# Hybrid attention step: the schedule of the cached samples changed from nine slots to ten, and the value products from two pages to four at a time

## What is computed

```python
k_full = cache_k[page_table[:, :own_page0]]
k_mean = jnp.mean(k_full.reshape(DB, n_full, MOBA_BLOCK, H, hd), axis=2)
gate = jnp.einsum('bqhd,bnhd->bhqn', qf, k_mean)
_, sel = lax.top_k(gate, top)                 # 3 of 4 blocks
# p: softmax over the selected pages and the new token
out = jnp.einsum('bhqk,bhqkd->bqhd', p, v_sel)
```

## Time and profile before

| | before |
|---|---|
| median of 3 runs | 469.26 us |
| span of the profiled execution, first to last instruction | 467.2 us |
| median less span (the profiled execution has no time of its own beside its span in the results; this stands for what lies around it) | 2.06 us |
| TensorE busy | 456.2 us (98%) |
| VectorE busy | 394.1 us (84%) |
| ScalarE busy | 294.4 us (63%) |
| GpSimd busy | 100.9 us (22%) |
| moved by DMA | 150.91 MB, mean 323 GB/s |

### The profile page before, as it was taken

How to read it: one execution, slowest core, us unless ns; L and a number is a source line. 1 busy time by engine, 2 the same in 40 slices (tenths; PEclk the granted TensorE clock), 3 DMA queues, 4 the chain that set the end, 5 groups by cost and what they waited for, 6 DMA issues and landing times.

```text
span 467.2 us, 11345 instructions
## 1 busy us (share of the span) xinstructions
PE 456.2 (98%) x3855; PEld 413.8 (89%) x3855; DVE 394.1 (84%) x1610; ACT 294.4 (63%) x490; POOL 100.9 (22%) x181
## 2 busy tenths in 40 slices
PE   6999999999999999999999999999999999999997
PEld 4899899897879888888899889899898898899997
DVE  3898899699999799999899999799999774668861
ACT  4966545686984496995486695666948357324430
POOL 2040421013323213423321332321223110000000
PEclk9999999999999999999999999999999999999999
DMA  8899699749999999999999999998999985457511
GB/s 304 322 353 407 183 322 371 240 158 340 317 416 408 404 368 354 412 410 408 408 380 315 409 412 409 411 372 303 382 415 409 410 334 188 149 180 261 182 48 48
DMA packets 44858, 150.91 MB, mean 323 GB/s; under 512 B 6192, under 2 KB 7796, under 8 KB 44672
## 3 DMA queue, kind: packets, MB, share of 16 engines
q1 hardware_dynamic: 20368, 70.77, 40.8%
q0 software_dynamic: 19008, 67.20, 37.3%
q10 hardware_dynamic: 5424, 12.21, 6.8%
HBM read 137.37 MB, written 12.76 MB: 321 GB/s over the span
## 4 chain that ended last, share of the span: by engine, by line
PE 70%; ACT 10%; DVE 10%; DMA 4%; issue 4%; ACTq 1%; POOLq 0%; SPq 0%; POOL 0%; DVEq 0%
PE pj L534 28%; PE pj L537 13%; PE wk L534 6%; PE pa L717 4%; PE wk L537 3%; DMA kpages<-in_cache_k 3%; DVE kpages L1170 3%; DVE wlo L1071 2%; ACT L838 2%; ACT whi L818 2%; PE wk L487 2%; DVE cslot L1252 2%; PE wk L639 2%; PE wk L673 1%; DMA cst<-in_consts 1%
## 5 line engine op out<-in xcount | busy, mean ns | idle before, releaser
L534 PE MATMUL pj<-xn,whi 128*128 128x264 f32 x1328 | 180.8, 288 | 1.6 <-ACT mqT L976 1.3
L534 PEld LDWEIGHTS pj<-xn,whi 128*128 128x128 f32 x1328 | 168.4, 189 | 10.2 <-issue 6.2
L1071 DVE TENSOR_TENSOR wlo<-wraw,whi 128x1024 fp32r<-128x1024 f32 x112 | 136.1, 1220 | 8.8 <-ACT whi L818 8.3
L818 ACT ACTIVATE whi<-wraw 128x1024 fp32r<-128x1024 f32 x112 | 117.9, 1053 | 23.1 <-PE wk L537 12.9
L1170 DVE CUSTOM_DVE_ANT_0 kpages<-kpages,qbc 128x128 f32<-128x128 f32 x512 | 115.5, 292 | 5.3 <-DMA kpages<-in_cache_k 5.1
L537 PE MATMUL pj<-xn,wlo 128*128 128x264 f32 x664 | 93.8, 284 | 0.4 <-DVE wlo L1071 0.4
L537 PEld LDWEIGHTS pj<-xn,wlo 128*128 128x128 f32 x664 | 85.5, 188 | 0.6 <-DVE wlo L1071 0.6
L404 POOL DMA_DIRECT2D kpages<-in_cache_k x64 | 34.3, 536 | 165.9 <-DVE sco L1170 141.9
L404 POOL DMA_DIRECT2D vpages<-in_cache_v x64 | 33.9, 530 | 57.9 <-issue 38.9
L1170 DVE DVE_READ_ACCUMULATOR2_ANT sco<- 128x1 f32 x512 | 42.8, 84 | 0.0
L717 PE MATMUL pa<-vpages,prob 128*32 128x256 f32 x512 | 34.2, 385 | 1.7 <-ACT prob L876 1.7
(11 more groups left out here) (271 smaller groups left out, 615.0 us busy)
## 6 DMA issues: line engine op xcount, KB each, us to landing
wraw<-in_weights SPq DMA_DIRECT2D x112, 512.0 KB, 6.8
kpages<-in_cache_k POOLq DMA_DIRECT2D x64, 512.0 KB, 8.1
vpages<-in_cache_v POOLq DMA_DIRECT2D x64, 512.0 KB, 10.8
cslot<-in_states SPq DMA_DIRECT2D x16, 512.0 KB, 9.4
out_C_s<-cslot ACTq DMA_DIRECT2D x16, 512.0 KB, 8.1
xres<-in_tokens SPq DMA_DIRECT2D x1, 1056.0 KB, 5.5
out_k_p<-kT ACTq DMA_DIRECT2D x4, 256.0 KB, 10.2
out_v_p<-v_nat ACTq DMA_DIRECT2D x4, 256.0 KB, 4.7
```

Of the source, the lines that this page charges most:

```text
L534: mm(bank[:, 0:T], whi[:, q, k, :], src[:, g, k, :], start=(k == 0 and g == 0), stop=False)
L818: A(whi[:, n % WSPLIT], wraw[:, n % WRAW], ACT.Copy).then_inc(whi_ready, 1)
L1071: V.tensor_tensor(wlo[:, n % WRAW], wraw[:, n % WRAW], whi[:, n % WSPLIT], ALU.subtract).then_inc(wlo_ready, 1)
```

## The change

The formula for the slots becomes tables. Samples start every 10 slots (2, 12, ... 72), so slots 8 and 9 of each sample have no key page. A visit has four pages, and there are two a sample: at 13 and 17 after the start; at 13 and 14 for the seventh sample (slots 75, 76), at 11 and 12 for the last one (slots 83, 84). The last sample has a shorter chain: SUMS at 8, SELECT 9, SHIFT and EXP 10, TOTAL 11, GATHER 13 (slot 85, as before). Value pages are loaded one a slot from slot 14 on, and two a slot for the last sample (slots 76 to 79). In the epilogue `token_scores` moves from step 12 to 18, its exponential from 14 to 19, `sample_totals` from 18 to 20. Each engine still executes the same operations; the matmuls of a value page are the same.

```diff
-START, PERIOD = 2, 9
-SUMS, SELECT, SHIFT, EXP, VALUES, TOTAL, GATHER = 9, 10, 11, 12, 13, 14, 20
-def due(g, lag):
-    b, left = divmod(g - START - lag, PERIOD)
-    return b if left == 0 and 0 <= b < NB else None
+STARTS = [2 + 10 * b for b in range(NB)]
+SUMS, SELECT, SHIFT, EXP, TOTAL, GATHER = range(6)
+LAGS = [(9, 10, 11, 12, 14, 20)] * (NB - 1) + [(8, 9, 10, 10, 11, 13)]
+VISITS = [(13, 17)] * (NB - 2) + [(13, 14), (11, 12)]
+VISIT = PAGES // 2
+LOADS = [[14 + p for p in range(PAGES)]] * (NB - 2) + [[14 + p // 2 for p in range(PAGES)]]
+def due(g, step):
+    for b in range(NB):
+        if g == STARTS[b] + LAGS[b][step]:
+            return b
+    return None
...
+def value_loads(g):
+    return [(b + 1) * PAGES + p for b in range(NB - 1) for p in range(PAGES) if g == STARTS[b] + LOADS[b][p]]
...
-                    for s in range(pair[0] * PAGES + 2 * pair[1] + VSLOTS, pair[0] * PAGES + 2 * pair[1] + VSLOTS + 2):
-                        if s < NB * PAGES:
-                            values(s)
+                for s in value_loads(g):
+                    values(s)
...
-                    for pg in (2 * pair[1], 2 * pair[1] + 1):
+                    for pg in range(VISIT * visit[1], VISIT * (visit[1] + 1)):
...
-                if i == 18:
+                if i == 20:
                     sample_totals()
...
-                if i == 14:
+                if i == 19:
                     act.wait_ge(ep_dve, 3)
...
-                if i == 12:
+                if i == 18:
                     token_scores()
```

More of the change, by code:

```diff
@@ L81, with value_visit @@
 LAST = BODY + 5 * KC
-START, PERIOD = 2, 9
-SUMS, SELECT, SHIFT, EXP, VALUES, TOTAL, GATHER = 9, 10, 11, 12, 13, 14, 20
-def due(g, lag):
-    b, left = divmod(g - START - lag, PERIOD)
-    return b if left == 0 and 0 <= b < NB else None
-def key_page(g):
[L97 to L106, removed]
-    return None
+STARTS = [2 + 10 * b for b in range(NB)]
[9 more added lines that the diff above has]
+    return None
+def key_page(g):
+    for b in range(NB):
+        if STARTS[b] <= g < STARTS[b] + PAGES:
+            return b * PAGES + g - STARTS[b]
+    return None
+def value_visit(g):
+    for b in range(NB):
+        for p, lag in enumerate(VISITS[b]):
+            if g == STARTS[b] + lag:
+                return b, p
+    return None
+def value_loads(g):
+    return [(b + 1) * PAGES + p for b in range(NB - 1) for p in range(PAGES) if g == STARTS[b] + LOADS[b][p]]
 class Chain:
@@ L470, in _ @@
                         spread_queries(s // PAGES + 1)
-                pair = value_pair(g)
-                if pair is not None:
-                    for s in range(pair[0] * PAGES + 2 * pair[1] + VSLOTS, pair[0] * PAGES + 2 * pair[1] + VSLOTS + 2):
-                        if s < NB * PAGES:
-                            values(s)
+                for s in value_loads(g):
+                    values(s)
                 if g % CHUNKS == 13 and g // CHUNKS + 1 < JOBS:
@@ L705, in cache_side @@
                     mm(page_sums[b % 2], ones, sco[:, b % 2].rearrange("p a h -> p (a h)"), start=True, stop=True).then_inc(g_ps, 1)
[L706 to L709, removed]
+                visit = value_visit(g)
+                if visit is not None:
+                    b = visit[0]
+                    if visit[1] == 0:
                         pe.wait_ge(prob_ready, b + 1)
                         pe.wait_ge(accr_ready, b)
-                    for pg in (2 * pair[1], 2 * pair[1] + 1):
+                    for pg in range(VISIT * visit[1], VISIT * (visit[1] + 1)):
                         s = b * PAGES + pg
```

## The result

The changed kernel takes 472.16 us (median of 4 runs, 471.65 to 473.26), the kernel before beside it 469.42 us. The ratio is 1.0061, 95% interval 1.0042 to 1.0080: 0.6% slower, where 1.2% faster was forecast, and outside the range of the prediction. Its profiled execution took 473.26 us, the longest of the four, with a span of 471.1 us; the forecast for the span was 461.4.

What follows compares the result with a forecast made beforehand. TensorE's own instruction list was taken as the path; 16 visits fewer at 0.33 us gave -5.3, and with +0.33 + 0.33 - 0.7 - 1.0 - 0.5 + 1.0 made -5.8 us: 463.5 us, range 460.8 to 467.8.

Steps and rivals of the forecast that it cites:

- the cost goes with the pages: Rival: 0.33 us belongs to the matmuls, not the turn, so merging visits gains nothing; 468.1 us, chance 0.04.
- Slot 15: First sample's visit and the project before it lose their waits for ScalarE and `wlo`: -1.0 us (bounds 0 and -1.1).
- the first boundary: Job boundary, slots 16 to 20: TensorE arrives 0.33 us earlier and waits 0.33 longer, nothing won: +0.33 us.
- The third boundary: Job boundary, slots 48 to 52: the 0.74 us wait for an exponential goes: -0.7 us (bounds 0 and -0.8).
- the second boundary: Job boundary, slots 32 to 36: slot 35's visit needs slot 34's exponential: +0.33 us (bounds 0 and +1.5).
- The two small waits of the epilogue: Waits at the seventh sample's first visit (0.3 us) and before the last sample's sums (0.2) go: -0.5 us.
- the last sample's chain: End of the epilogue: sums to visit, 7.2 us of work fits in 8.8 us: 0 (bounds 0 and +1.5).
- the value page of slot 76: Epilogue: TensorE waits for the seventh sample's page 7, loaded in slot 73 behind a key page: +1.0 us.
- The rival of the starved end: Rival: seventh sample's value loads queue behind key pages, up to 9.5 us wait at slot 76; 472.0 us, chance 0.08.
- the body otherwise: Visits at 25, 35, 45, 55 follow their exponential by one slot; nothing added, at most 0.74 us each.
- the first rival: The rival "the neighbours take the body's gain"; its sign was `wlo` with more than 2 us among TensorE's waits.
- the neighbours take the body's gain: Rival: in the body, waits for `wlo` or an evacuation fill each visit saved; 467.8 us, chance 0.17.

Runs made afterwards that it cites:

- experiment 6: Experiment 5 plus the next job's rows of decays and floors loaded one slot earlier, ahead of that slot's value page: 466.10 us, ratio 0.9934.
- experiment 8: The changed kernel with only the next job's rows of decays and floors loaded one slot earlier: 470.44 us, ratio 1.0023.
- experiment 9: Experiment 6 plus the seventh sample's second visit in slot 77 instead of 76, the last sample's value loads moved behind it: 465.05 us, ratio 0.9913.
- experiment 4: The changed kernel with the sixth sample's first visit in slot 66 instead of 65, its loads following, and the token product in slot 70 instead of 67: 473.98 us.
- experiment 3: The changed kernel with the first six samples back at four visits of two pages: 472.25 us, ratio 1.0053.
- experiment 1: The changed kernel with value pages 5 to 7 of the seventh sample all loaded in slot 71, ahead of the next key pages: 469.05 us, ratio 0.9986.
- experiment 5: The changed kernel with the edits of experiment 1 and experiment 4 together: 468.61 us, ratio 0.9988.
- experiment 2: The kernel before, nine slots to a sample kept, with two visits of four pages in place of four of two: 468.68 us, ratio 0.9982.
- experiment 7: Experiment 5 with the first five samples back at four visits of two pages: 469.82 us, ratio 1.0009.
- experiment 10: Experiment 9 plus the third sample's first visit in slot 36 instead of 35, its loads a slot later: 467.04 us, ratio 0.9951.
- experiment 11: The kernel before with only the next job's rows of decays and floors loaded one slot earlier: 470.06 us, ratio 1.0021.

## Why the prediction was wrong

**Term by term.** TensorE's own arithmetic held: a project with a visit of four pages and the project behind it take 4.88 + 3.03 us, less two projects 2.05, forecast 1.72 + 0.33. That ends the rival "the cost goes with the pages", by which it would be twice 1.19. The reason given against this rival was not sound, though: four passes in 0.215 us are 129 cycles each at 2.4 GHz, less than half of the 293 that each of a project's 24 matmuls of 264 columns takes (2.93 us in all). So the passes ran side by side, and their spacing doesn't show what a single one costs. Slot 15 lost both its waits (forecast -1.0; the slot is 1.4 us shorter beyond the pages). At the first boundary the wait is 1.29 us where it was 0.66, and slot 20 starts 0.3 us earlier, slot 16 already 0.5: nothing won there, as forecast. The third boundary's gain came: the third job has no idle time at all (70.05 of 70.05 us). At the second the visit of slot 35 waits 1.5 us for the exponential once the rows are out of the way (experiments 6, 8 and 9), the upper bound of that term and not its +0.33. The two small waits of the epilogue went, and the last sample's chain came in time (its parts as listed add up to 6.0 us and not 6.4, which only widens the room).

**The step that failed in size** is the value page of slot 76, +1.0 us in the sum. Its issue came 7.2 us after the start of slot 73 (363.50 to 370.70; I had 5.2 to 8.2 and took the early end), its landing took 11.4 us (I took 10 where the earlier trace rows have 12.1 for a median), and it was needed 15.3 us after that start. I had 14.4, with a slip: three pages are 3 x 0.43 = 1.3 us by my own price, not 0.65. That makes 7.2 + 11.4 - 15.3 = 3.3 us, and the visit 3.9 us longer. I had taken the favourable end of two quantities at once. That a late issue brings a late landing is not shown: the page was issued at 370.11, 370.70 and 371.51 in experiment 4, the changed kernel and experiment 3, and took 12.0, 11.4 and 11.6 us. With the slower project behind it, which I had not priced at all, the page cost 5.0 us in the execution profiled. Taking it away (experiment 1) gave 3.1 us by the medians. The rival of the starved end had the mechanism and the place, not the size: it needed 6.8 us to turn the sign alone.

**The steps that were missing** are three. The exponential of slot 64 came behind the gate's evacuations: 1.5 us. The token product of slot 67: the slot takes 5.15 us where it took 3.17, 2.0 us. The rows of the middle job: 2.35 us by the difference between its 74.13 us and the 71.78 of experiment 9. The page was 4.0 above its term. Together 4.0 + 1.5 + 2.0 + 2.35 = 9.85 us, against 471.1 - 461.4 = 9.7 us missed. That they meet so closely is in part luck: taken away one by one they don't give these amounts (experiments 4, 5 and 8). At the second boundary I had put only the chain of ScalarE and written of the body otherwise "Nothing added"; I had looked at what a visit waits for, and not at the small row loads that share GpSimd's queue with the pages, though the change moves the page loads around them. The sign that I had named for the first rival, more than 2 us of waits for `wlo`, came true with 2.9 us and yet misled: moving the rows alone took both waits away (experiment 8), so it was a late load and not VectorE's own work. The low end of the range, 460.8, had a slip too: it counts 0.8 us won at the first boundaries, for which no row stands; without it the sum gives 461.6.

**Was TensorE's list the path?** Only in part, and this is the sentence at the head of the prediction that fails: "TensorE's own instruction list is the path". The other engines do not "stand a little behind it": the runs show that what catches up is the larger part. Merging alone is worth 0.7 us of 5.3 in the kernel before (experiment 2), undoing it costs 0 of 4.0 in the changed kernel (3) and 1.2 to 1.5 of 3.3 in experiment 5's (7). The rival "the neighbours take the body's gain" was right for the merging alone. With the ten-slot period VectorE has 1.3, 6.0 and 3.4 us less to do in the three jobs, and two of them then kept their 2.2 and 2.4 us. So it seems that the gain needs both parts, the turns saved and the page work thinned, and after that a place for each transfer; the ten-slot period with no merging at all was not run, and experiment 3 is the nearest to it.

Experiment 9, with the late page and the late rows gone, has a span of 462.9 us, 1.5 above the 461.4 forecast. It is 8.2 under the changed kernel's: 2.35 in the middle job, 6.0 behind slot 64. That these waits stood between is shown by experiments 1, 6, 8 and 9. Where the last 1.5 us lie is only argued: experiment 9 still waits 1.5 us at slot 35, 1.2 for `wlo` in slot 68 and 0.6 for scores in slot 80, of which the sum had 0.33.

What stays open: why a wait of TensorE is followed by a slow project in some executions and not in others. How much it makes can be read where both kinds are on record: 1.7 us between the two groups' medians in experiment 5, 1.1 in experiment 1. It is not all of the spread: the kernel before goes from 468.5 to 471.6 us without it.

## What to carry to other kernels

Where three engines and the DMA are all near full, don't price a saved microsecond on the busiest one at a microsecond: here 0.7 of 5.3 us came through where the others had been given no room, and 1.2 to 1.5 of 3.3 where VectorE had some. Then look for the transfer whose landing hangs on another engine's list: what is won ahead of it is waited away at it. When a change moves large loads in a queue, list every small load that stands in the same queue, with who waits for it. Where a wait is issue plus landing minus need, take the late ends together, not the median of each.

## What the runs showed of the hardware

A wait of TensorE can cost more than its length. The project behind it took 4.15 us instead of 3.03 after 3.28 us (granted clock 0.69 over it), 4.5 after 1.82 in experiments 1 and 10 (0.62) and after 2.65 in experiment 3 (0.64), 4.6 after 1.27 and 0.64 in experiment 7 (0.63). After 1.44 and 1.82 us in the changed kernel it took 3.01 and 2.99. How often it happens goes with the schedule. The mean granted clock of an execution is under 0.997 in 4 of 4 executions of the changed kernel, 6 of 6 in experiments 3 and 4, 11 of 12 in 8, 6 of 12 in 1, 5 of 12 in 10, 4 of 12 in 5, 2 of 12 in 7 and 11, and none in experiments 2, 6 and 9 or in 75 of the kernel before.

Loads of 1 KB issued between 512 KB pages on GpSimd's queue were there 9.9 us after the second one's issue in the changed kernel, and 7.4 in the kernel before (185.55 to 192.99); a slot earlier, in experiment 6, it was at most 7.7 us (177.19 to 184.86), and VectorE did not yet want them.

A page's landing hardly moved with TensorE: 382.13, 382.08 and 383.15 us in the changed kernel and experiments 4 and 3, where TensorE stood ready for it at 378.8, 379.2 (after 2.25 us for the page in front) and 382.3. It took 11.4 to 12.0 us from its issue, at 391 to 401 GB/s over the 30 us from 352 to 382.
